# Second block: tile halves in two buffers in turn, each tile split behind its residual add, and the attention bias read back from shifted rows

## What is computed

```python
def second_block(x, ...):
    h = x
    for layer in range(2):
        if layer == 0:
            h = h + gla_mixer(rmsnorm(h, ln_mix[0]), ..., w_out)   # gated linear attention
        else:
            kb, vb = shared_kv(rmsnorm(h, kv_norm), w_kv)
            h = h + swa_mixer(rmsnorm(h, ln_mix[1]), kb, vb, w_q, sinks, rel_table, w_out)
        h = h + sq_relu_mlp(rmsnorm(h, ln_mlp[layer]), w_up, w_down)
    return rmsnorm(h, ln_final)

def swa_mixer(...):    # window of 128, 16 query heads, 2 key/value heads
    s = q @ k.T * 64 ** -0.5
    bias = rel_table[bucket(i + 128 - j)]      # depends on i - j alone: (16 heads, 128, 256)
    s = where(mask, s + bias, -1e30)
    ...                                        # softmax with a sink logit, times v

rmsnorm(x, g) = x * rsqrt(mean(x * x) + eps) * g
```

## Time and profile before

| | |
|---|---|
| median of 3 runs | 2555.11 us (2554.48 to 2556.16) |
| profiled execution | 2556.41 us, of which the span shown is 2554.6 us |
| TensorE matmul busy | 2465.3 us, 97% |
| VectorE busy | 1469.0 us, 58% |
| ScalarE busy | 876.1 us, 34% |
| mean granted TensorE clock | 0.986 of full speed |
| DMA | 226.09 MB, mean 89 GB/s |

### The profile page before, as it was taken

The page is one execution under the profiler, slowest core; times in us unless marked ns, Lnnn a source line. Parts: engine busy times, 40 slices in busy tenths (PEclk is TensorE's granted clock), DMA queues, the critical chain, the costliest instruction groups (busy, mean ns, idle before and its releaser), DMA issues.

```text
span 2554.6 us, 28913 instructions
## 1 busy us (share of the span) xinstructions
PE 2465.3 (97%) x11338; PEld 2003.8 (78%) x11338; DVE 1469.0 (58%) x2020; ACT 876.1 (34%) x1161; POOL 9.9 (0%) x23
## 2 busy tenths in 40 slices
PE   8999999999999899999998999999999999999998
PEld 7888777788887787788886687778888777788886
DVE  6888635644445734544446534566666665566666
ACT  3344543422223633422223434322222554322222
POOL 0000000000000000000000000000000000000000
PEclk9999999999999999999999999999999999999999
DMA  5222221322222211222222221232222211222221
GB/s 185 88 83 83 94 80 66 101 97 99 99 99 82 83 66 66 83 99 98 89 94 86 83 90 42 68 118 97 99 99 98 69 65 54 96 98 89 93 98 66
DMA packets 32924, 226.09 MB, mean 89 GB/s; under 512 B 3765, under 2 KB 3797, under 8 KB 6480
## 3 DMA queue, kind: packets, MB, share of 16 engines
q1 hardware_dynamic: 31536, 220.21, 25.3%
q0 software_dynamic: 1312, 4.81, 0.5%
HBM read 222.89 MB, written 2.12 MB: 88 GB/s over the span
## 4 chain that ended last, share of the span: by engine, by line
PE 87%; DVE 8%; ACT 3%; issue 1%; DMA 0%; DVEq 0%; SPq 0%; ACTq 0%
PE bank L668 86%; DVE w_lo L1809 2%; ACT w_hi L1293 1%; DVE xs L1885 1%; DVE cacc L1995 1%; ACT xs L1355 1%; ACT xh L1306 1%; DVE xs L1899 1%; PE bank L1238 0%; DVE hs L2046 0%; DVE xs L1861 0%; DVE xl L1817 0%; DVE gs L2046 0%; DVE sum_x L1828 0%; PE bank L929 0%
## 5 line engine op out<-in xcount | busy, mean ns | idle before, releaser
L668 PE MATMUL bank<-xh,w_hi 128*128 128x512 f32 x1960 | 777.9, 397 | 43.8 <-DVE xl L1818 11.9
L668 PE MATMUL bank<-xl,w_hi 128*128 128x512 f32 x1960 | 769.4, 393 | 0.0
L668 PE MATMUL bank<-xh,w_lo 128*128 128x512 f32 x1960 | 769.3, 392 | 0.0
L1809 DVE TENSOR_TENSOR w_lo<-w_raw,w_hi 128x2048 fp32r<-128x2048 f32 x205 | 469.5, 2290 | 395.2 <-ACT w_hi L1293 394.7
L1293 ACT ACTIVATE w_hi<-w_raw 128x2048 fp32r<-128x2048 f32 x205 | 391.2, 1909 | 398.3 <-PE bank L668 398.2
L668 PEld LDWEIGHTS bank<-xh,w_hi 128*128 128x128 f32 x1960 | 371.8, 190 | 138.2 <-issue 34.5
L668 PEld LDWEIGHTS bank<-xl,w_hi 128*128 128x128 f32 x1960 | 372.1, 190 | 78.1 <-issue 1.9
L668 PEld LDWEIGHTS bank<-xh,w_lo 128*128 128x128 f32 x1960 | 371.7, 190 | 78.2
L1861 DVE TENSOR_TENSOR xs<-xs,bank 128x512 f32<-128x512 f32 x448 | 294.0, 682 | 115.5 <-PE bank L668 114.4
L668 PE MATMUL bank<-mhh,w_lo 128*128 128x512 f32 x512 | 199.2, 389 | 0.0
L668 PE MATMUL bank<-mhh,w_hi 128*128 128x512 f32 x512 | 199.2, 389 | 0.0
(11 more groups left out here) (263 smaller groups left out, 2517.6 us busy)
## 6 DMA issues: line engine op xcount, KB each, us to landing
w_raw<-weights_in SPq DMA_DIRECT2D x205, 1024.0 KB, 4.8
xs<-x_in SPq DMA_DIRECT2D x4, 512.0 KB, 6.7
sf<-rel_scratch POOLq DMA_DIRECT2D x1, 2048.0 KB, 12.0
y_out<-xs SPq DMA_DIRECT2D x8, 256.0 KB, 2.0
w_raw<-weights_in SPq DMA_DIRECT2D x2, 512.0 KB, 5.7
mk<-mem_in POOLq DMA_DIRECT2D x1, 1024.0 KB, 9.3
window<-consts_in POOLq DMA_DIRECT2D x1, 576.0 KB, 4.0
sum_q<-consts_in POOLq DMA_DIRECT2D x1, 256.0 KB, 9.2
```

Source lines behind the costliest of these rows:

```text
L668: return pe.matmul(dst, a, b, start=start, stop=stop)
L1809: dve.tensor_tensor(w_lo[:, c % 2, :], w_raw[:, c % 2, :], w_hi[:, c % 2, :].bitcast(F32), ALU.subtract)\
```

## The change

The two pairs of buffers take turns. What was read from `xh`/`xl` by mlp0 is now in `yh`/`yl`, then `sk` and `sv` read `xh`/`xl`, `sq` reads `yh`/`yl`, `so` reads `xh`/`xl`, and mlp1 `yh`/`yl`. Since the buffer that is written is not the one that is being read, a tile's halves are made right behind its residual add, and `late_high` and `late_rest` are gone. Behind mlp0 the squares for the norm now come after the halves with the gain `kvn` and after the split of `sv`'s unit, and the norm's sums on TensorE come after `sk`.

The bias row is stored 128 times in DRAM (3 MB in place of 24 KB), with its sign changed, and is read back with a row step of 383 elements in place of 384 - so row p starts p elements earlier - straight into `bias`. The eight products with `flip`, their eight drains and the load of `flip` are gone.

```diff
-    scratch = nc.dram_tensor("rel_scratch", [16, 384], F32, kind="Internal").ap()
+    scratch = nc.dram_tensor("rel_scratch", [16, P, 384], F32, kind="Internal").ap()
...
             const(kk[0:33, 0, 0:384], "onehot", onehot_loaded, 33)
-            const(flip[:, :], "flip", flip_loaded)
             wait_drained(pool, ("vec", 0))
-            pool.dma_start(scratch, vt[0:16, 0:384]).then_inc(vec_stored, 16)
+            pool.dma_start(scratch, vt[0:16, 0:384].unsqueeze(1).broadcast_to([16, P, 384])).then_inc(vec_stored, 16)
             pool.wait_ge(vec_stored, 16)
-            hankel = bass.AP(tensor=scratch.tensor, offset=0, ap=[[1, P], [384, 16], [1, 2 * P]])
-            pool.dma_start(sf[:, :].rearrange("p (h k) -> p h k", h=16), hankel).then_inc(hankel_loaded, 16)
+            shifted = bass.AP(tensor=scratch.tensor, offset=127, ap=[[383, P], [P * 384, 16], [1, 2 * P]])
+            pool.dma_start(bias[:, :, :], shifted).then_inc(bias_loaded, 16)
...
# TensorE
-            pe.wait_ge(hankel_loaded, 16)
-            pe.wait_ge(flip_loaded, 16)
-            bias_tile(0)
-            bias_tile(1)
-            feature_unit("sk", 0, ytile, ready=kv_ready)
-            for m in range(2, 8):
-                bias_tile(m)
+            feature_unit("sk", 0, ready=tile_ready)
+            rms_norm_sums("r2")
...
-            feature_unit("sq", 0, ready=tile_ready)
+            feature_unit("sq", 0, ytile, ready=tile_ready)
...
# ScalarE, residual behind go and so
                         wait_drained(act, keys[k])
-                        if k == KT - 1 and gain:
-                            late_high(gain, keys[k], range(1))
+                        if gain:
+                            high(k, xs[:, k, :], col(gain, k), yh)
                         square(k, xs[:, k, :])
-                if gain:
-                    late_high(gain, keys[KT - 1], range(1, KT))
...
# ScalarE, behind mlp0's last unit
                     wait_drained(act, (name, "last", "d", k))
-                    square(k, xs[:, k, :])
+                    if name == "mlp0":
+                        high(k, xs[:, k, :], col("kvn", k))
+                    else:
+                        square(k, xs[:, k, :])
...
             chunks("mlp0")
-            wait_full(act, ("mlp0", "last", "d", KT - 1))
+            split_hi(UNITS["sk"] + 1)
+            for k in range(KT):
+                square(k, xs[:, k, :])
             for k in range(KT):
-                high(k, xs[:, k, :], col("kvn", k), yh)
-            drain_bias(0)
-            drain_bias(1)
+                high(k, xs[:, k, :], col("mix2_g1", k), yh)
             rms_stats("r2")
-            high(0, xs[:, 0, :], col("mix2_g1", 0))
-            high(1, xs[:, 1, :], col("mix2_g1", 1))
-            split_hi(UNITS["sk"] + 1)
-            for k in range(2, KT):
-                drain_bias(k)
-                high(k, xs[:, k, :], col("mix2_g1", k))
             split_hi(UNITS["sv"] + 1)
...
# VectorE, residual behind go and so
                         sums_behind(k, keys, has_mean)
+                    for k in (2 * j, 2 * j + 1) if gain else ():
+                        give(rest(k, xs[:, k, :], col(gain, k), yh, yl), "tile_ready")
...
# VectorE, behind mlp0's last unit
                     add(k, keys[k])
-                    sums_behind(k, keys, has_mean)
-                split_lo(c + 1)
+                    if name == "mlp0":
+                        if k == 1:
+                            split_lo(c + 1)
+                        if k:
+                            wait_drained(dve, keys[k - 1])
+                            give(rest(k - 1, xs[:, k - 1, :], col("kvn", k - 1)), "tile_ready")
...
+                split_lo(c + 2 if name == "mlp0" else c + 1)
...
             chunks("mlp0", False)
+            for k in range(1, KT - SUMMED):
+                add_to_sums(k, False, xs_at)
             for k in range(KT):
-                give(rest(k, xs[:, k, :], col("kvn", k), yh, yl), "tile_ready")
+                give(rest(k, xs[:, k, :], col("mix2_g1", k), yh, yl), "tile_ready")
             mean_square(("r2", "sq"), D)
```

More of the change, by code:

```diff
@@ L96, in constants @@
     put("ident", (i == j).astype(np.float32))
-    put("flip", (i + j == 127).astype(np.float32))
     put("mask32", ((i <= j) & (i // 32 == j // 32)).astype(np.float32))
@@ L310, in plan_banks @@
     chunks("mlp0", False)
-    for m in range(2):
-        fill(("bias", m), 4 + m % 2)
     norm("r2", False)
     pairs("sk", 1)
-    for m in range(2, 8):
-        fill(("bias", m), 4 + m % 2)
     fill(("sv", 0, 0), 2 * (UNITS["sv"] % 2), UNITS["sv"])
@@ L1157, in _ @@
             chunks("mlp0", tile_and_sums("r1"))
-            pe.wait_ge(hankel_loaded, 16)
-            pe.wait_ge(flip_loaded, 16)
-            def bias_tile(m):
-                wait_free(pe, ("bias", m))
-                full(mm(bank(("bias", m))[:, :], flip[:, :], sf[:, m * T:(m + 1) * T], True, True), ("bias", m))
-            def kv_ready(k):
-                tile_ready(k)
-                if k == 3:
-                    rms_norm_sums("r2")
-            bias_tile(0)
-            bias_tile(1)
-            ytile = lambda k: (yh[:, k, :], yl[:, k, :])
-            feature_unit("sk", 0, ytile, ready=kv_ready)
-            for m in range(2, 8):
-                bias_tile(m)
+            feature_unit("sk", 0, ready=tile_ready)
+            rms_norm_sums("r2")
             c = UNITS["sv"]
@@ L1179, in _ @@
             for k in range(KT):
-                last = mm3(bank(("sv", 0, 0))[:, :], weights(c, k * P, P), ytile(k), k == 0, k == KT - 1)
+                last = mm3(bank(("sv", 0, 0))[:, :], weights(c, k * P, P), xtile(k), k == 0, k == KT - 1)
             full(last, ("sv", 0, 0))
@@ L1382, in residual @@
                         wait_drained(act, keys[k])
-                        if k == KT - 1 and gain:
-                            late_high(gain, keys[k], range(1))
+                        if gain:
+                            high(k, xs[:, k, :], col(gain, k), yh)
                         square(k, xs[:, k, :])
-                if gain:
-                    late_high(gain, keys[KT - 1], range(1, KT))
                 if norm:
                     mean_stats(norm, n, split=behind(norm))
-            def late_high(gain, last_key, tiles=range(KT)):
-                wait_full(act, last_key)
-                for k in tiles:
-                    high(k, xs[:, k, :], col(gain, k))
             def chunks(name, final_squares=True):
@@ L1838, in xs_at, with residual @@
                 return xs[:, k, :]
-            def residual(keys, c0, n_units, has_mean, alpha=None, first=0):
+            def residual(keys, c0, n_units, has_mean, alpha=None, first=0, gain=None):
                 for j in range(n_units):
@@ L1920, in scale_residual @@
                 steps.wait()
-            def late_rest(gain, l):
-                for k in range(KT):
-                    give(rest(k, xs[:, k, :], col(f"{gain}_g{l}", k)), "tile_ready")
             def chunks(name, has_mean):
@@ L2367, in _ @@
             steps.wait()
-            for m in range(8):
-                wait_drained(dve, ("bias", m))
+            dve.wait_ge(bias_loaded, 16)
             def swa(it):
@@ L2412, in _ @@
                 swa(it)
-            residual(pair_keys("so"), UNITS["so"], 4, False, first=1)
-            late_rest("mlp2", 1)
+            residual(pair_keys("so"), UNITS["so"], 4, False, first=1, gain="mlp2_g1")
             mean_square(("r3", "sq"), D)
```

47 lines of the change are left out of this document (23 added, 24 removed).

## The result

The changed kernel takes **2559.39 us** (median of 20 runs, 2557.85 to 2560.96) beside 2555.07 us for the kernel before, on the same chip: ratio 1.0016, 95% interval 1.0010 to 1.0022. It is 4.3 us slower, within the 0.2% that the prediction calls no change, and not the forecast 2548.4; the range ended at 2552.0. The profiled span is 2558.4 us beside 2554.6.

The account below looks back on a forecast made before the run. TensorE, with work in 97% of the span, was taken as the bound. Gains 0 + 2.6 + 4.1 = 6.7 us took the profiled 2556.41 to 2549.7; the median, 1.3 lower, was forecast at 2548.4 us, range 2544.5 to 2552.0.

Parts of the forecast that it names:

- Place 1: From go to mlp0: TensorE's 2.5 us idle stays, since the load of `kk` releases it; gain 0.
- Place 3: From so to mlp1: 2.57 us of idle and 1.5 us of slow matmuls go; gain 4.1 us.
- Place 2: From mlp0 to sq: sq starts 4.6 us earlier, less 2.0 us for a low clock; gain 2.6 us.
- The bias's transfers: Store and read-back of the bias: store taken as 18 us, weight loads still in time; cost 0.
- the worst load of the run took 10.3 us: Slowest weight load in the kernel before, against 4.8 us at the median; used to argue that the store costs 0.
- ScalarE's `w_hi` waiting for a load in mlp0: One of the listed signs that would show the prediction wrong; no size given.
- the sum would stay the same: Claim that a store of an estimated 30 us in place of 18 would leave the total gain unchanged.
- 16.4 us of room: Time from a weight load's issue at 1671.9 to when it is wanted at 1688.37.
- the store starves the weight loads: Rival: loads share DMA engines with the bias store and come late; 36 us, 2584 us; chance 5%.
- (L - 16.4)/2: That rival's TensorE wait in each unit when a load takes L > 16.4 us, since two slots take turns.
- 20 units at L = 20: That rival's case: some 20 weight units during the store, each load 20 us; 36 us in all.
- the upper bound of 230 us: Store's time if reckoned as 128 times the 24 KB store of 1.8 us; the forecast took 18 us instead.

Follow-up runs that it names:

- the early load: Changed kernel with its store in eight pieces, plus the one-hot matrix loaded some 100 us earlier into a free buffer: 2545.72 us.
- the half store: Kernel before plus an extra, unread 1.5 MB store from 16 partitions (64 copies in place of 128): 2556.02 us, ratio 1.0002.
- new halves alone: Kernel before with only the change's new tile halves; bias the old way (24 KB store, eight `flip` products, eight drains): 2551.13 us, ratio 0.9986.
- the kernels with a spare store: Kernel before plus one extra, unread store: 3 MB from 16 partitions 2566.63 us, half of that 2556.02 us, 3 MB from 128 partitions 2555.33 us.

## Why the prediction was wrong, point by point

- **Place 1**, gain 0: right. The wait for the load of `kk` is 2.39 us, before 2.36; the early load shows that nothing else held the place.
- **Place 3**, 2.57 + 1.5 = 4.1: right. From so's last matmul to the norm's sums it was 7.06 us, now 2.95, 4.1 less, at full clock.
- **Place 2**, 4.6 - 2.0 = 2.6: right, term by term. 4.9 us earlier, with waits of 0.8 (forecast 1.1) ahead of the sums and 4.4 (4.7) ahead of sq; 12 slow matmuls cost 5.11 - 2.76 = 2.35 (2.0).
- **The bias's transfers**, 0: wrong, and this alone made the prediction wrong. They cost 10.3 us in mlp0, against the 6.6 that places 2 and 3 gave. Three things there failed. The store's time: 18 us by the rate of a read that goes to 128 partitions; it took 34.7. Its effect: "the worst load of the run took 10.3 us" was the row for a load beside a fast transfer, and I let it stand for one beside a slow one; it was 24.2. ScalarE's `w_hi` waiting for a load in mlp0, which the prediction names as a sign of being wrong, is the row at 1696.67. And the sentence that the sum would stay the same at an estimated 30 us: the half store shows that already 17 us are at the threshold. The Trainium skill ("SBUF — State Buffer", section on the DMA port swizzle, 104 GB/s for partitions 0 to 15) was nearer than the row I took: 3.15 MB in 34.7 us are 91 GB/s. The lesson is in what was wanted from the number: with 16.4 us of room, any store of more than about 17 us that holds the DMA engines is a case of its own, and both values that I had lay above that.
- **The rival** "the store starves the weight loads" is what happened, and its threshold of 16.4 us held. Its formula, (L - 16.4)/2, did not: at L = 17.6 it gives 0.6 us where 0.7 was measured, but that is luck, for at 24.2 it gives 3.9 where TensorE waited 7.2. Nor did its price: it took 20 units at L = 20 from the upper bound of 230 us. In a store of 34.7 us two loads fall, and only the first one's excess shows, 24.2 - 16.4 = 7.8, since the second runs while everything waits for the first. With the slow matmuls 10.3 us in place of 36. Its chance of 5% was far too low: "a store from few partitions is unlike any row" was a reason for a wide range.
- What I had not seen at all did no harm to the number: sq had to wait for two things, the split and, until 2.8 us earlier, sk's banks. It would have misled anyone who mends the one named.

## What to carry to other kernels

A DMA that reads few partitions is not a small load on the others because it moves few GB/s. Here the store from 16 partitions kept the DMA engines 94% busy or more in the windows read beside a load, so compare its duration, not its bytes, with the room that the other transfers have; spread it over 128 partitions or cut it in pieces shorter than that room. When a wait is to be removed, list everything that its first waiting instruction needs (operands, weights, the PSUM bank) with the time of each, for the profile names only the last. Idle time ahead of a stage can cost slow matmuls behind it as well, and where it did, removing it paid about one and a half times (2.3 us of idle gave 3.95, 4.5 gave 6.9).

## What the runs showed of the hardware

- The same 3 MB stored to DRAM: 34.7 and 34.1 us out of 16 partitions (91 GB/s), 11.5 us out of 128 (274 GB/s); nearly the same amount out of another tile of 128 partitions 14.4 us; half of it out of 16 partitions 17.3 us, an eighth 5.4 us.
- A 1 MB weight load on another queue took 4.9 us at the median, 21 to 24 beside the 3 MB store from 16 partitions, and at most 9.8 beside 3 MB from 128 partitions (14.9 where eight reads of 16 partitions each followed), with the DMA engines over 90% busy in the same window of both stores.
- TensorE's clock fell from 2.4 to 1.2 GHz behind idle times of 2.3 to 2.4 us (places 1 and 3), 4.4 and 7.2 us. In the changed kernel the granted clock over the 5 us behind was 0.67 at place 1, 0.52 behind 4.4 us and 0.50 behind 7.2 us. There 12 to 13 matmuls took 1.7, 2.35 and 2.7 us too much, and 1.5 at place 3 before. Behind 1.9 us (new halves alone) it was 1.7.
- The length of the idle time alone does not tell what it costs. Behind the same 2.02 us ahead of sk, 12 matmuls took 2.8 us in the kernel before and in two of the kernels with a spare store, at a granted clock of 1.00, and 4.42 us in the one with half the store, at 0.60. Behind 0.8 to 0.9 us nothing was lost.
